# Routed blocks made of two half blocks of two experts, plain stores of the results and a gather of each token's rows at the end

## The reference

```
scores = sigmoid(h @ w_router)                     # 576 x 64
top_idx = top_k(scores + router_bias, 8)
top_w = scores[top_idx] / sum(scores[top_idx]) * 2.5
for each token and each of its 8 experts e:
    y += top_w * ((silu(h @ gate[e]) * (h @ up[e])) @ down[e])    # gate, up 1024 x 256, down 256 x 1024
y += swiglu(h, shared expert)
x = x + gate_f * RMSNorm(y)
```

## Time and profile before

| what | us |
|---|---|
| median of 3 runs | 1939.59 (1939.55 to 1946.28) |
| the profiled execution, its own time | 1928.52 |
| span of its instructions | 1926.5 |
| PE busy in the span | 1719.2 (89%) |
| DVE, ACT, POOL busy | 448.2, 349.2, 302.3 |
| bytes moved by DMA | 452.28 MB |

### The profile page before, as it was taken

How to read it: one execution, slowest core, us unless ns; L and a number is a source line. 1 busy time by engine, 2 the same in 40 slices (tenths; PEclk the granted TensorE clock), 3 DMA queues, 4 the chain that set the end, 5 groups by cost and what they waited for, 6 DMA issues and landing times.

```text
span 1926.5 us, 20976 instructions
## 1 busy us (share of the span) xinstructions
PE 1719.2 (89%) x6443; PEld 1038.6 (54%) x6444; DVE 448.2 (23%) x975; ACT 349.2 (18%) x796; POOL 302.3 (16%) x464
## 2 busy tenths in 40 slices
PE   4499999898989999997877999999999999999991
PEld 1167888776657777644443444444444444444440
DVE  1120000357611111145561111111111111111114
ACT  1110000356400000033111111111111111111111
POOL 0110060002000000010002222222222222222220
PEclk7699999769989999997988999999999999999996
DMA  7862498524987434410118999998898999999976
GB/s 268 348 226 29 68 336 284 180 94 134 302 266 242 152 107 127 139 61 17 44 56 325 335 298 338 323 341 264 311 340 282 337 296 335 332 344 335 345 243 185
DMA packets 140301, 452.28 MB, mean 235 GB/s; under 512 B 10955, under 2 KB 75979, under 8 KB 111420
## 3 DMA queue, kind: packets, MB, share of 16 engines
q1 hardware_dynamic: 117853, 331.36, 48.5%
q0 software_dynamic: 22400, 120.25, 22.0%
HBM read 395.96 MB, written 100.36 MB: 258 GB/s over the span
## 4 chain that ended last, share of the span: by engine, by line
PE 67%; DMA 20%; SPq 5%; DVE 4%; issue 2%; ACT 1%; POOL 0%; ACTq 0%; POOLq 0%; DVEq 0%
PE bank L1924 63%; DMA arena<-in_we_up 14%; SPq L748 1%; PE bank L2419 1%; DMA arena<-in_cache_b 1%; PE bank L2089 1%; PE bank L2130 1%; PE bank L2434 1%; DMA arena<-in_w_ada 1%; DMA arena<-in_w_in 1%; DMA arena<-h2rows,icol 1%; DMA mods<-arena 1%; SPq L923 1%; SPq L922 1%; SPq L898 1%
## 5 line engine op out<-in xcount | busy, mean ns | idle before, releaser
L1924 PE MATMUL bank<-arena 128*128 (+11 forms) x5184 | 1574.8, 497 | 110.3 <-ACTq L1314 36.3
L1924 PEld LDWEIGHTS bank<-arena 128*128 128x128 f32 (+4 forms) x5184 | 883.5, 196 | 698.6 <-issue 535.8
L1074 POOL DMA_INDIRECT yacc<-arena,scol x70 | 112.1, 1602 | 366.8 <-DVE arena L1888 361.7
L1883 DVE TENSOR_TENSOR arena<-bank,arena 128x256 f32<-128x256 f32 x70 | 29.7, 424 | 509.8 <-ACT arena L1344 509.8
L1091 ACT ACTIVATE arena<-bank 128x512 f32<-128x512 f32 (+6 forms) x151 | 74.8, 506 | 342.9 <-PE bank L1924 216.9
L1888 DVE TENSOR_SCALAR arena<-bank,wcol 128x512 f32<-128x512 f32 x70 | 52.5, 751 | 198.3 <-PE bank L1924 198.3
L1344 ACT ACTIVATE arena<-bank 128x256 f32<-128x256 f32 x70 | 26.8, 383 | 391.8 <-issue 221.2
L2419 PE MATMUL bank<-ident,arena 128*128 128x128 f32 x560 | 78.1, 283 | 20.9 <-DMA arena<-h2rows,icol 15.4
L2419 PEld LDWEIGHTS bank<-ident,arena 128*128 128x128 f32 x560 | 71.6, 193 | 43.4 <-issue 19.8
L1383 DVE COPY arena<-bank 128x512 f32<-128x512 f32 (+6 forms) x71 | 42.2, 603 | 205.7 <-PE bank L1924 175.2
L1059 POOL DMA_INDIRECT arena<-h2rows,icol x70 | 70.7, 1010 | 60.2 <-POOL icol L1056 56.7
(11 more groups left out here) (249 smaller groups left out, 667.0 us busy)
## 6 DMA issues: line engine op xcount, KB each, us to landing
arena<-in_we_gate SPq DMA_DIRECT2D x64, 1024.0 KB, 7.0
arena<-in_we_up SPq DMA_DIRECT2D x64, 1024.0 KB, 11.4
arena<-in_we_down SPq DMA_DIRECT2D x64, 1024.0 KB, 7.7
out<-in_cache_b POOLq DMA_DIRECT2D x8, 4080.0 KB, 15.1
arena<-in_w_ada SPq DMA_DIRECT2D x12, 2048.0 KB, 17.5
arena<-in_cache_b SPq DMA_DIRECT2D x18, 1024.0 KB, 8.7
arena<-in_w_in SPq DMA_DIRECT2D x7, 2048.0 KB, 15.4
arena<-in_w_in SPq DMA_DIRECT2D x24, 512.0 KB, 7.0
```

Source lines behind the costliest of these rows:

```text
L1074: pool.indirect_dma_start(yacc[j], bass.IndirectOffsetOnAxis(ap=scol[:, j:j + 1], axis=0), yb[:, j, :], None, compute_op=ALU.add).then_inc ...
L1924: return pe.matmul(out, lhsT, rhs, start=first, stop=last)
```

## The change

Each expert's rows are padded to a multiple of 64, not 128, so that a block of 128 rows holds two half blocks, which may be of two experts. In each matmul of the loop, partitions 0 to 63 of the result come from the first half's 64 columns of the left operand and the first half's weights, and partitions 64 to 127 from the other 64 columns and the second half's weights: two matmuls of 64 columns each, where there was one of 128. The second half's weights must lie in a place of their own, since the two can be one expert or two, so DVE copies gate and up (4096 columns) and ACT copies down (2048 columns) of the second half's expert from the ring into `whalf[j]` before each block. The weights lie in a ring of four buffers, not two. Experts 0, 1 and 2 are loaded before the tables are there, expert 3 behind them, and all 64 are loaded in order.

The results are not scaled and not accumulated. POOL stores each block plainly to its own 128 rows of `yrows`. After the loop it gathers for each of 5 tiles and each of 8 choices the rows of its tokens (40 indirect DMAs, 12 buffers), and DVE multiplies each by its weights and adds it to the shared expert's result in one instruction. That result waits in HBM (`yshared`) meanwhile. So that no row of `yrows` is undefined, POOL first copies 35 blocks' worth of `w_out` into its upper part (5 DMAs, 18.35 MB). The tables are built otherwise: the weights in an earlier place, the one-hot blocks with 70 columns, not 200, and partly by ACT.

```
-NBLK = (TOK * TOPK + NE * (P - 1)) // P // 2 * 2 + 2
+HALF = P // 2
+NBLK = -(-(TOK * TOPK + NE * (HALF - 1)) // P)
+NBLK += 2 + NBLK % 2
+RING = 4
...
+        RING_AT = (A_W0, A_W1, 0, A_W0 + 6144)
+        wexp = [at(n, 6144) for n in RING_AT]
+        whalf = [at(n, 6144) for n in (A_W1 + 6144, A_M)]
...
+            def expert_weights(n, e, done):
                 if done is not None:
                     sp.wait_ge(gu_done, done)
-                sp.dma_start(wexp[j][:, 0:2048],
-                             we_gate[0, e].rearrange("a (p k) n -> p (a k n)", k=KD)).then_inc(wgu_in[j], 16)
-                sp.dma_start(wexp[j][:, 2048:4096],
-                             we_up[0, e].rearrange("a (p k) n -> p (a k n)", k=KD)).then_inc(wgu_in[j], 16)
+                    sp.sem_inc(load_ticks, 1)
+                sp.dma_start(wexp[n][:, 0:2048],
+                             we_gate[0, e].rearrange("a (p k) n -> p (a k n)", k=KD)).then_inc(wexp_in[n], 16)
+                sp.dma_start(wexp[n][:, 2048:4096],
+                             we_up[0, e].rearrange("a (p k) n -> p (a k n)", k=KD)).then_inc(wexp_in[n], 16)
                 if done is not None:
                     sp.wait_ge(d_done, done)
-                sp.dma_start(wexp[j][:, 4096:6144],
-                             we_down[0, e].rearrange("a (p k) n -> p (a k n)", k=2)).then_inc(wd_in[j], 16)
+                    sp.sem_inc(load_ticks, 1)
+                sp.dma_start(wexp[n][:, 4096:6144],
+                             we_down[0, e].rearrange("a (p k) n -> p (a k n)", k=2)).then_inc(wexp_in[n], 16)
+            for h in range(2):
+                sp.wait_ge(fills_done, INDEX[("mix", TILES - 1, h)] + 1)
+            expert_weights(0, slice(0, 1), None)
+            expert_weights(1, slice(1, 2), None)
             for t in range(TILES):
                 wait_emptied(sp, ("sy", t, 1))
-                sp.dma_start(yacc[0][toks(t), :], ysh[0:parts(t), t, :]).then_inc(yacc_in, 16)
-                if t == 0:
-                    sp.wait_ge(zeros_ready, 1)
-                sp.dma_start(yacc[1][toks(t), :], yb[0:parts(t), 1, :]).then_inc(yacc_in, 16)
+                sp.dma_start(yshared[toks(t), :], ysh[0:parts(t), t, :]).then_inc(ysh_out, 16)
+            expert_weights(2, slice(2, 3), None)
             sp.wait_ge(tables_ready, 1)
...
+            wait_fill(pool, ("ga", 6, 1))
+            for n in range(YMIN, NBLK + 1, KD):
+                m = min(KD, NBLK + 1 - n)
+                pool.dma_start(yrows[P * n:P * (n + m), :], w_out[0, 0:P * m, :]).then_inc(yrows_set, 16)
...
-                    pool.wait_ge(y_out[j], 16 * i + 16)
-                    pool.tensor_copy(scol[:, j:j + 1], addrow[:, bass.ds(2 * i + j, 1)]).then_inc(cols_ready, 1)
-                    pool.tensor_copy(wcol[:, j:j + 1], wtab[:, bass.ds(2 * i + j, 1)]).then_inc(cols_ready, 1)
-                pool.wait_ge(cols_ready, 4 * i + 4)
-                for j in range(2):
                     pool.wait_ge(y_act, 2 * i + j + 2)
                     pool.wait_ge(y_dve, 2 * i + j + 2)
                     pool.sem_inc(gather_ticks, 1)
-                    pool.indirect_dma_start(yacc[j], bass.IndirectOffsetOnAxis(ap=scol[:, j:j + 1], axis=0),
-                                            yb[:, j, :], None, compute_op=ALU.add).then_inc(y_out[j], 16)
+                    pool.dma_start(yrows[bass.ds(2 * P * i + P * j, P), :], yb[:, j, :]).then_inc(y_out[j], 16)
+            pool.wait_ge(d_done, 2 * n_pairs + 2)
+            for j in range(2):
+                pool.wait_ge(y_out[j], 16 * n_pairs + 16)
+            pool.wait_ge(weights_idle, 1)
+            pool.sem_inc(gather_ticks, 1)
+            for n, (t, k) in enumerate(gathers()):
+                r = parts(t)
+                if n >= GBUFS:
+                    pool.wait_ge(g_used, n - GBUFS + 1)
+                pool.indirect_dma_start(gbuf[n % GBUFS][0:r, :], None, yrows,
+                                        bass.IndirectOffsetOnAxis(ap=rowi[0:r, TOPK * t + k:TOPK * t + k + 1], axis=0)
+                                        ).then_inc(g_in[n % GBUFS], 16)
...
+            def weights_wait(r):
+                due = [act.value_load(blocki[0:1, bass.ds(r + (DUE + NBLK * n), 1)], min_val=1, max_val=NE // RING + 1)
+                       for n in range(RING)]
+                for n in range(RING):
+                    act.wait_ge(wexp_in[n], 48 * due[n])
                 act.sem_inc(weights_in, 1)
-            weights_wait(loads_due(0))
+            def copy_down(j, r):
+                base = act.value_load(blocki[0:1, bass.ds(r + NBLK, 1)], min_val=0, max_val=A_W1)
+                act.activation(whalf[j][:, 4096:6144], arena[:, bass.ds(base + 4096, 2048)],
+                               ACT.Copy).then_inc(d_copied, 1)
+            act.wait_ge(ysh_out, 16 * TILES)
+            weights_wait(0)
+            copy_down(0, 0)
+                weights_wait(2 * i + 1)
+                copy_down(1, 2 * i + 1)
...
+                turned(0)
                 exps(1)
-                turned(1, second)
+                turned(1)
                 result(0)
-                following = loads_due(2 * i + 2)
+                weights_wait(2 * i + 2)
+                copy_down(0, 2 * i + 2)
...
+            def copy_gate_up(j, r):
+                dve.wait_ge(weights_in, r + 1)
+                base = dve.value_load(blocki[0:1, bass.ds(r + NBLK, 1)], min_val=0, max_val=A_W1)
+                dve.tensor_copy(whalf[j][:, 0:4096], arena[:, bass.ds(base, 4096)]).then_inc(gu_copied, 1)
+            dve.wait_ge(ysh_out, 16 * TILES)
+            copy_gate_up(0, 0)
             with dve.Fori(0, n_pairs) as i:
                 for j in range(2):
                     dve.wait_ge(t_done, 2 * i + j + 3)
                     dve.tensor_copy(xT[:, j, 512:1024], psb[2 * j + 1][:, :]).then_inc(xt_dve, 1)
+                copy_gate_up(1, 2 * i + 1)
                 for j in range(2):
-                    e, a = (act3[:, 3 * j + n, :] for n in (0, 2))
                     dve.wait_ge(e_ready, 2 * i + j + 1)
-                    dve.tensor_tensor(a, psb[4 + j][:, FF:2 * FF], e, ALU.mult).then_inc(a_ready, 1)
+                    dve.tensor_tensor(act3[:, 2 * j + 1, :], psb[4 + j][:, FF:2 * FF], act3[:, 2 * j, :],
+                                      ALU.mult).then_inc(a_ready, 1)
                 for j in range(2):
                     dve.wait_ge(y_out[j], 16 * i + 16)
                     dve.wait_ge(d_done, 2 * i + j + 3)
-                    dve.wait_ge(cols_ready, 4 * i + 2 * j + 2)
-                    dve.tensor_scalar(yb[:, j, 512:1024], psb[7 if j == 0 else 3][:, :], wcol[:, j:j + 1], None,
-                                      ALU.mult).then_inc(y_dve, 1)
-            def both(t):
+                    dve.tensor_copy(yb[:, j, 512:1024], psb[7 if j == 0 else 3][:, :]).then_inc(y_dve, 1)
+                    if j == 0:
+                        copy_gate_up(0, 2 * i + 2)
+            def gathered(t):
                 r = parts(t)
-                dve.wait_ge(f_in[t], 32)
-                dve.tensor_tensor(ysh[0:r, t, :], ysh[0:r, t, :], yother[0:r, t, :], ALU.add).then_inc(f_sum, 1)
-            both(0)
+                for k in range(TOPK):
+                    n = TOPK * t + k
+                    dve.wait_ge(g_in[n % GBUFS], 16 * (n // GBUFS + 1))
+                    if k:
+                        dve.wait_ge(g_used, n)
+                    dve.scalar_tensor_tensor(ysh[0:r, t, :], gbuf[n % GBUFS][0:r, :], wts[0:r, t, k:k + 1],
+                                             ysh[0:r, t, :], ALU.mult, ALU.add).then_inc(g_used, 1)
+            dve.wait_ge(ysh_in, 16 * TILES)
+            gathered(0)
...
+                    pe.wait_ge(gu_copied, 2 * i + j + 1)
+                    wv, wh = (w[:, 0:4096].rearrange("p (j k n) -> p k j n", j=2, k=KD) for w in (weights[j], whalf[j]))
                     for k in ks:
-                        ins = mm(psb[4 + j][:, :], xT[:, j, P * k:P * (k + 1)], wv[:, k], k == 0, k == KD - 1)
+                        mm(psb[4 + j][0:HALF, :], xT[:, j, P * k:P * k + HALF], wv[:, k], k == 0, k == KD - 1)
+                        ins = mm(psb[4 + j][HALF:P, :], xT[:, j, P * k + HALF:P * (k + 1)], wh[:, k],
+                                 k == 0, k == KD - 1)
                     return ins
...
+                    pe.wait_ge(d_copied, 2 * i + j + 1)
                     to = psb[(6 if j == 0 else 2) + h]
                     for k in range(2):
                         c = 4096 + D * k + 512 * h
-                        ins = mm(to[:, :], aT[:, j, k * P:(k + 1) * P], weights[j][:, c:c + 512], k == 0, k == 1)
+                        mm(to[0:HALF, :], aT[:, j, k * P:k * P + HALF], weights[j][:, c:c + 512], k == 0, k == 1)
+                        ins = mm(to[HALF:P, :], aT[:, j, k * P + HALF:(k + 1) * P], whalf[j][:, c:c + 512],
+                                 k == 0, k == 1)
                     return ins
```

311 lines of the change are left out of this document (154 added, 157 removed).

## The result

The changed kernel takes 1949.0 us (median of 17 runs, 1936.4 to 1957.2), the kernel before 1936.6 on the same chips (17 runs). The ratio is 1.0057, 95% interval 1.0038 to 1.0075: slower by about half a per cent, where 1834 us was forecast, with a range of 1775 to 1900. The profiled execution has a span of 1947.3 us.

A forecast was written before the change was run, and what follows sets the result against it. PE was taken as the bound, with the weights' supply just behind. 1018 us to the first gate matmul, 722 of loop and 81 behind it gave a span of 1821, 1823 with 2 around it, scaled by 1.0057 to 1834; range 1775 to 1900.

The forecast's parts named there:

- Strips side by side: Loop matmuls: two of 64 columns run beside each other and cost what one full matmul did, nothing added.
- The two rivals on strips: Loop matmuls: strips overlap in part, 1965 us (1948 by the skill's share), chance 0.07; no overlap, 2271 us, chance 0.04.
- Durations of the copies: Loop, second half's weights: DVE's 4096 columns take 2.3 us a block, ACT's 2048 about 2.0 us.
- Their place: Loop copies: block 1's lie under gate_up(0), block 0's under down(1), hidden at 2.3 us; on the path if weights are late.
- The pair without a wait: Loop: a pair of blocks with no wait takes 23.9 us, 0.6 us of it for changes between full and split form.
- 7.3n + 9 for a pair: Loop: a pair with n new experts needs 7.3n us of load and about 9 us of SP standing still.
- The clock: Loop: waits of 7 us and more cost PE some 0.7 us each at the slower clock, 8 us.
- "Cost nothing" for the fill: Ahead of the loop: filling yrows, 18.35 MB, costs nothing, as slowed loads are not yet due; without that cover perhaps 10 us.
- The first gather: Ahead of the loop: the first transposes wait 5 us (0 to 7) for their gather, sharing engines with one expert's loads.
- The tail: Behind the loop: 81 us, 39 more than before, mostly DVE's 40 multiply-adds at 1.32 us, 53 us.
- the rival with strips that overlap in part: Loop matmuls: at 1.3 a pair's 20.6 us grow by 6.2, 131 us in all, 1965 us; chance 0.07.
- The sign that the prediction itself named for being wrong: Loop: a pair of over 28 us with all weights in, one of several signs listed as showing the forecast wrong.

The follow-up runs named there:

- the reads early: Changed kernel, with ACT and DVE reading the next block's registers right behind block 1's copy, under gate_up(0): 1896.8 us, ratio 0.9806 to the kernel before.
- The blocks in turn: Changed kernel with registers read early and the yrows filling spread; PE finishes block 0, down included, before gate_up(1): 1841.4 us, ratio 0.9518.
- An eighth of the bytes: Changed kernel with seven eighths of the experts' weights left out, 16 of 128 partitions loaded: 1861.2 us, ratio 0.9621.
- early reads and an eighth of the bytes: Changed kernel with registers read early and only 16 of 128 partitions of the experts' weights loaded: 1770.3 us, ratio 0.9163.
- early reads and spread fill: Changed kernel with registers read early and the yrows filling issued in five parts behind cache copies: 1874.4 us, ratio 0.9692.
- the last version: On the blocks in turn with block 1's transposes behind gate_up(0), the next pair's block 0 transposes moved behind gate_up(1): 1803.6 us, ratio 0.9330.

## Why the prediction was wrong, step by step

**Strips side by side: right.** 32 records of 64 columns take what 16 of 128 columns took the earlier trace rows, so nothing is added (the chain of waits, one `gate_up` of a pair):

```profile
1072.32 7.04 PE bank L1966 x32
```

For three strips the Trainium skill, "TensorE: Matmul & The Clock Gate", Part 3, has a speedup of 2.38, a share of 0.79; for two strips of 64 columns such a loss does not show: the overlap is whole. The two rivals on strips fall. That 1949 lies near the 1948 and 1965 of one of them is a coincidence.

**Durations of the copies: right** (2301 against 2300 ns, where the working's own pace and fixed part give 2.4 us; 1912 against 2000). **Their place: half right.** Hidden in short pairs; in long ones they cost about 20 us together, for which the sum had nothing.

**The pair without a wait: the working left out a term.** 23.9 us was right for the work (24.2 with the reads early), but in the changed kernel a short pair takes 28. The prediction listed DVE's and ACT's copies between `result(0)` and `result(1)` and gave the register reads in front of them no time: four due counts and a base, 3 us on ACT's queue with the waits. Before, two due counts were read there, and the wait and the other engines' work on it stood behind `result(1)`. With 3.4 us of cover, 1.9 of copy fits and 3.0 + 1.9 does not. By the loops with and without, 814 and 767 us, this is 47 us: half of the 92 that the loop is above the forecast.

**7.3n + 9 for a pair: wrong in form.** Alone among short pairs, a pair with three new experts is hidden by the ring (pair 3: 24.2 with early reads, the rule says 31). In a row they cost more than the rule: 34 to 42 at n = 3, 44 at n = 4. With the reads early, the eight long pairs (5, 6, 18, 19, 21 to 24) take 309 us where the rule gives 255; the four others with n = 3 take 105 where it gives 124, and the thirteen with n = 1 or 2 take 328 for 311. That is the other half of the 92, with the 8 us of the clock taken off. The 9 us of standing still were read in a kernel whose PE rarely waited. Here the standing holds PE's own wait for the weights of block 1: 24.0 us from gate to down, of which two loads fill 4.9. So each late load makes the next one late. The blocks in turn break this link: SP stands 5.6 us in the like place, and seven of the eight long pairs fall to 27.4 to 28.6 with all the bytes loaded. An eighth of the bytes in the old order takes them away too, so it is the two together that make them. What share PE's order has, what share the later place of ACT's and DVE's waits, and what share the one semaphore for all three loads was not tried apart.

**The clock: 8 us was too little.** It came from 0.7 us for each long wait; the rows give 57 us in the loop, with waits in every pair. It is a consequence of the two steps above, lies inside their 92 us and not beside them, and came back with them (50 us less PE time with the blocks in turn).

**"Cost nothing" for the fill: wrong.** 17 us. The cover named, that the mixing stage's loads were not yet due, failed for the second half of `w_out`; the price named without cover, 10 us, was too small too.

**The first gather: wrong.** It was to land in 5 us. Behind the tables PE still waits 11.3:

```profile
1026.67 1.00 PE L1966 MATMUL bank<-ident,arena 128*1 128x70 f32 x14
1038.97 1.97 PE L2461 MATMUL bank<-ident,arena 128*128 128x128 f32 x8 [11.29 <-DMA arena<-h2rows,icol]
1043.25 1.94 PE L2461 MATMUL bank<-ident,arena 128*128 128x128 f32 x8 [2.31 <-DMA arena<-h2rows,icol]
```

SP reached expert 2 only at 1022.6, behind the five stores to `yshared`, and expert 3 at 1028.5, so the gathers share the engines with two experts again. The working's own two terms give 1015, not 1018 (1027 less 4 and less 7.9). To that come the fill with 14.7, the gathers with 8.6 (11.3 and 2.3, less 5), and 7 us by which the profiled execution already issued the load of the first half of `w_out` later than that of the kernel before (718.15 for 711.15): 1045, as measured. The 7 us are no effect of the change: with early reads, and with early reads and an eighth of the bytes, where the program is the same up to there, that load is issued at 712.11 and 711.95. Executions differ by this much, and the forecast's factor of 1.0057 allows for it.

**The tail: right to 7 us.** DVE is the bound; the last store takes 8.7 us to land where 5 were taken:

```profile
1868.86 0.99 POOL L1101 DMA_INDIRECT arena<-yrows,arena  x1 [8.73 <-DMA yrows<-arena]
1875.26 11.00 DVE L1936 SCALAR_TENSOR_TENSOR arena<-arena,wts 128x1024 f32<-128x1024 f32 x8 [16.43 <-DMA arena<-yrows,arena]
```

Eight multiply-adds in 11.0 us are 1.37 each, where 1.32 was taken.

One slip in the sums changes nothing: five sixths of 26 x 6.2 are 134 us, not 131, so the rival with strips that overlap in part stood at 1968.

Every term that was wrong as a whole lengthens the time. The sign that the prediction itself named for being wrong, a pair of over 28 us with all weights in, is what came: with an eighth of the bytes thirteen of the 25 pairs are above 28. The range was built from the size of unknown operations; strips and copies came out well, and what a store takes of the DMA engines' time no run tells apart. It had no room for an error in the queues.

## What to carry to other kernels

Price everything that stands in an engine's queue between two instructions of the path, register reads too: they hold no engine busy and are in no group of the profile, but five of them cost 3 us in each pair. When a loop's supply is released by its own progress, ask what the release waits for: if the releasing instruction stands behind one that waits for the same supply, a late load feeds the next. Then the order of the consumer can be changed where the bytes cannot; giving up 3 us of overlap in each pair took the eight longest behind the first from 306 us, in the kernel with early reads and spread fill, to 229 together. Ask also what a shared semaphore adds: a wait for three loads ends with the last of them, though the work behind it may need only the first two.

## What the hardware showed beside it

POOL's issue of a gather takes 1.00 us, but 2.96 where DVE's copy of 4096 columns runs beside it, in the last version:

```profile
1242.67 2.29 DVE L1920 COPY arena<-arena 128x4096 f32 x1 [0.23 <-ACTq L1356]
1242.87 2.96 POOL L1082 DMA_INDIRECT arena<-h2rows,icol  x1 [0.81 <-POOL icol L1079]
1262.16 1.00 POOL L1082 DMA_INDIRECT arena<-h2rows,icol  x1 [0.81 <-POOL icol L1079]
```

(The Trainium skill, "SBUF — State Buffer", on who interferes with whom, has DVE and GpSimd share a pair of ports, which a copy in a two-port mode holds until its end; the rows agree: the issue beside the copy ends 0.9 us behind it. In which mode the copy ran no row shows.) A plain store of 512 KB, estimated at 1.3 us of the engines' time, takes 8.3 us from issue to landing in the changed kernel's loop, and 4.0 beside an eighth of the weights' bytes; with early reads these are 10.9 and 4.9. A transfer from DRAM to DRAM of 18.35 MB lengthened one load of 2 MB from 7.7 to 55.0 us, which the DMA shares of those stages before, 0.17 and 0.63, did not foretell.
